# A landing semaphore for each expert slot, two expert loads in flight, and a published count for the engines

## The reference

```python
def moe(h, w_router, b_router, w_eg, w_eu, w_ed):
    scores = jax.nn.sigmoid(logits)            # logits = h @ w_router
    sel = scores + b_router
    grp_score = jnp.sum(lax.top_k(grp, TOP_K)[0], axis=-1)
    best = jnp.argmax(grp_score, axis=-1)      # one of 4 groups of 4 experts
    _, idx = lax.top_k(masked, TOP_K)          # two experts of that group
    ...
    gate = jnp.einsum('btd,edf->btef', h, w_eg)
    up = jnp.einsum('btd,edf->btef', h, w_eu)
    a = jax.nn.silu(gate) * up * combine[..., None]
    return jnp.einsum('btef,efd->btd', a, w_ed)
```

## Time and profile before

| | us |
|---|---|
| median of 3 runs | 1204.32 |
| lowest and highest | 1196.26, 1206.15 |
| the profiled execution | 1205.71 |
| its span, first to last instruction | 1203.7 |
| PE busy (share) | 1050.0 (87%) |
| DVE busy (share) | 670.2 (56%) |
| ACT busy (share) | 412.2 (34%) |
| POOL busy (share) | 202.6 (17%) |
| mean granted clock of TensorE | 0.927 |

### The profile page before, as it was taken

One profiled execution on the slowest core, in us unless ns is written; L12 is line 12 of the kernel. 1 busy time (PEld: TensorE's weight loads), 2 busy tenths in 40 slices (PEclk: granted clock), 3 DMA queues, 4 the chain that ended last, 5 costly groups with the idle time before them and its releaser, 6 DMA issues.

```text
span 1203.7 us, 18160 instructions
## 1 busy us (share of the span) xinstructions
PE 1050.0 (87%) x5952; PEld 798.1 (66%) x5953; DVE 670.2 (56%) x1125; ACT 412.2 (34%) x803; POOL 202.6 (17%) x244
## 2 busy tenths in 40 slices
PE   5899999999999999789878999983599989979950
PEld 2599999989999875569874555543366656646640
DVE  3431887141797138319985333356666766567644
ACT  3342322252222242535662101110244444344413
POOL 2200000000000021002354000000224324324324
PEclk9599999999999999799998999995699999989985
DMA  9543333223342132122125322208448888887848
GB/s 351 204 142 122 139 139 140 89 80 116 137 157 99 60 136 77 39 88 63 53 45 228 114 95 105 105 36 296 175 145 241 293 265 247 277 271 201 243 65 349
DMA packets 58643, 187.37 MB, mean 156 GB/s; under 512 B 7874, under 2 KB 20658, under 8 KB 52450
## 3 DMA queue, kind: packets, MB, share of 16 engines
q1 hardware_dynamic: 46100, 142.29, 33.0%
q0 software_dynamic: 7920, 28.84, 10.4%
q10 hardware_dynamic: 4576, 15.62, 3.4%
HBM read 151.53 MB, written 35.21 MB: 155 GB/s over the span
## 4 chain that ended last, share of the span: by engine, by line
PE 71%; DVE 13%; DMA 7%; issue 3%; ACT 3%; POOL 1%; ACTq 1%; SPq 0%; DVEq 0%; POOLq 0%
PE psum L1242 35%; PE psum L1184 27%; DMA RB<-in_w_exp 2%; PE psum L1461 2%; DVE RW L1725 2%; DMA RB<-in_x_sample 2%; PE psum L1123 2%; DVE RE L1752 1%; DMA acc_scratch<-RE,idxsc 1%; DMA out<-RB 1%; DVE RE L1760 1%; PE psum L1396 1%; PE psum L1199 1%; PE psum L1168 1%; DMA RW<-gm_scratch 1%
## 5 line engine op out<-in xcount | busy, mean ns | idle before, releaser
L1184 PE MATMUL psum<-input_parts,weight_parts 128*128 128x320 f32 x2208 | 340.9, 313 | 1.7 <-DVE input_parts L1560 1.7
L1184 PEld LDWEIGHTS psum<-input_parts,weight_parts 128*128 128x128 f32 x2208 | 326.9, 189 | 10.6 <-issue 6.9
L1242 PE MATMUL psum<-RB,RW 128*128 x324 | 147.9, 607 | 1.5 <-issue 1.3
L1567 DVE TENSOR_TENSOR weight_parts<-RW,weight_parts 128x1024 fp32r<-128x1024 f32 x46 | 56.3, 1224 | 164.8 <-ACT weight_parts L854 164.8
L854 ACT ACTIVATE weight_parts<-RW 128x1024 fp32r<-128x1024 f32 x46 | 48.7, 1058 | 238.2 <-PE psum L1184 238.0
L1242 PE MATMUL psum<-expert_parts 128*128 128x512 f32 x486 | 126.5, 413 | 1.9 <-DVE expert_parts L1989 1.9
L1242 PEld LDWEIGHTS psum<-expert_parts 128*128 128x128 f32 x486 | 91.3, 188 | 32.4 <-issue 14.8
L1242 PEld LDWEIGHTS psum<-RB,RW 128*128 128x128 f32 x324 | 61.2, 196 | 69.4 <-issue 69.4
L1242 PE MATMUL psum<-RS,RB 128*128 128x512 f32 (+1 forms) x200 | 79.9, 554 | 2.7 <-DMA RS<-in_wpw 1.5
L673 POOL TENSOR_TENSOR RE<-RE,RA 2x2304 f32<-2x2304 f32 (+1 forms) x2 | 9.5, 4762 | 404.9 <-DMA RA<-in_b_ada 404.9
L1242 PE MATMUL psum<-RC,RB 128*128 128x512 f32 x160 | 72.5, 607 | 0.0
(11 more groups left out here) (325 smaller groups left out, 1498.3 us busy)
## 6 DMA issues: line engine op xcount, KB each, us to landing
RB<-in_w_exp SPq DMA_DIRECT2D x48, 1024.0 KB
RW<-in_w_ada SPq DMA_DIRECT2D x48, 512.0 KB, 3.5
RW<-in_w_in SPq DMA_DIRECT2D x46, 512.0 KB, 4.1
RW<-gm_scratch SPq DMA_DIRECT2D x20, 256.0 KB, 3.4
h_scratch<-RE SPq DMA_DIRECT2D x10, 512.0 KB, 2.6
acc_scratch<-RA SPq DMA_DIRECT2D x10, 512.0 KB, 3.6
RB<-acc_scratch ACTq DMA_DIRECT2D x10, 512.0 KB, 7.3
out<-RB SPq DMA_DIRECT2D x10, 512.0 KB, 2.7
```

The lines of the kernel that those rows point to most:

```text
L1184: last = nc.tensor.matmul(psum[:, 2 * r + g, 0:GW], spl[:, r, wv, k], hT[:, xv, k, g * GW:(g + 1) * GW], start=(k == 0 and wv == 0 and xv ...
L1242: return nc.tensor.matmul(out, lhsT, rhs, start=start, stop=stop, **kw_)
L1567: nc.vector.tensor_tensor(spl[:, r, 1], raw[:, r], spl[:, r, 0].bitcast(F32), ALU.subtract).then_inc(wlo_ok, 1)
```

## The change

The three parts of a load now add to a semaphore of their slot, `w_land0` to `w_land2`. Nobody but SyncE waits on these. When SyncE finds that a slot's load has landed, it adds 48 to `w_full` by an empty instruction (`publish`). The other engines' code is unchanged: they wait on `w_full` as before. SyncE no longer waits for the landing of load n-1 before it issues load n, but issues load n when its slot is free and then waits for load n-1 and publishes it. Loads 0 and 1 are issued together; load 15 is followed by the publications of experts 14 and 15. The first pass of the loop is written out.

```diff
+    w_land = [sem(f"w_land{r}") for r in range(3)]
...
-        def load_expert(r, src, came):
-            if came is not None:
-                sp.wait_ge(w_full, came)
+        def load_expert(r, src):
             for q in range(WPART):
-                sp.dma_start(wexp[:, r * WE + q * WP:r * WE + (q + 1) * WP], src[:, q * WP:(q + 1) * WP]).then_inc(w_full, 16)
+                sp.dma_start(wexp[:, r * WE + q * WP:r * WE + (q + 1) * WP], src[:, q * WP:(q + 1) * WP]).then_inc(w_land[r], 16)
+
+        def publish(r, landed):
+            sp.wait_ge(w_land[r], landed)
+            nc.sync.nop().then_inc(w_full, 16 * WPART)
 
         sp.wait_ge(lg_ps, NT)
         for e in range(2):
-            load_expert(e, a["w_exp"][e], 16 * WPART * e if e else None)
+            load_expert(e, a["w_exp"][e])
+        publish(0, 16 * WPART)
         sp.wait_ge(route_ok, 3)
...
-        load_expert(2, listed(slice(2, 3)), 16 * WPART * 2)
-        with sp.Fori(1, NE // 3) as i:
+        load_expert(2, listed(slice(2, 3)))
+        publish(1, 16 * WPART)
+        publish(2, 16 * WPART)
+
+        def refill(n, free, r):
+            done = sp.value_load(endI[0:1, free], min_val=1, max_val=NBLK)
+            src = listed(n)
+            sp.wait_ge(dn_ps, done)
+            load_expert(r, src)
+
+        for r in range(3):
+            refill(slice(3 + r, 4 + r), slice(r, r + 1), r)
+            if r:
+                publish(r - 1, 2 * 16 * WPART)
+        with sp.Fori(2, NE // 3) as i:
             for r in range(3):
-                done = sp.value_load(endI[0:1, bass.ds(i * 3 + (r - 3), 1)], min_val=1, max_val=NBLK)
-                src = listed(bass.ds(i * 3 + r, 1))
-                sp.wait_ge(w_full, i * (48 * WPART) + 16 * WPART * r)
-                sp.wait_ge(dn_ps, done)
-                load_expert(r, src, None)
+                refill(bass.ds(i * 3 + r, 1), bass.ds(i * 3 + (r - 3), 1), r)
+                publish((r - 1) % 3, i * (16 * WPART) + (16 * WPART if r else 0))
         done = sp.value_load(endI[0:1, NE - 4:NE - 3], min_val=1, max_val=NBLK)
         src = listed(slice(NE - 1, NE))
         sp.wait_ge(dn_ps, done)
-        load_expert(0, src, 16 * WPART * (NE - 1))
+        load_expert(0, src)
+        publish(2, 5 * 16 * WPART)
+        publish(0, 6 * 16 * WPART)
```

## The result

The changed kernel took 1239.02 us, median of 4 runs (1234.78 to 1242.77), against 1200.29 us for the kernel before in the same comparison. The ratio is 1.0288, 95% interval 1.0246 to 1.0330: slower by some 35 us. A second comparison on another occasion gave 1.0301 (1.0235 to 1.0366), with medians of 1237.54 and 1203.49, 34.1 us apart.

A forecast was written before the change was run, and what follows sets the result against it. The MoE loop was taken as bound by TensorE. New stalls 28.5, plus 4.1 at expert 7, minus 0.7 at expert 11, gave +31.9 us: 1205.7 to 1237.6, for the median 1236; range 1227 to 1246.

The forecast's parts named there:

- Part 1: SyncE's loads in the MoE loop: removing the wait for the previous landing gains 0 on the path, at most 15.6 us.
- Part 2: Publication behind the next refill: TensorE idles 7.4 us at the transposes where the expert ahead has one block; +31.9 us overall.
- The block behind a stall: MoE loop: the next block after a stall runs 2.1 us over its 10.35 us period, bounds 1.3 and 2.6.
- Which experts: Experts with one-block predecessors pay: 4, 10, 13 by 9.5 us each, 7 by +4.1, 11 by -0.7.
- expert 2 spared: Before the loop: expert 2's publication follows its own load without a refill between, long before block 3 wants it; no cost.
- The pair at 10 and 11: Blocks 16, 17: expert 10's new stall lets load 11 land earlier; expert 11's stall costs 9.5 instead of 10.2, -0.7 us.
- A full stall: At a late block's transposes: 7.4 us idle plus 2.1 us for the slower next block, 9.5 us, between 8.5 and 11.1.
- the two old stalls: Kernel before, late landings of loads 7 and 11: stalls costing 5.4 and 10.2 us, 15.6 us together.
- The one without the clock: Rival at the loop's stalls: gaps come but the clock falls no more often than now; +26 us, 1230; chance 0.11.
- The one in which the clock stays low: Rival: the whole next block or more after each of five stalls runs at lower clock; 15 us on top, 1251; chance 0.08.

The follow-up runs named there:

- The seven late publications: Changed from the kernel before: experts 3, 5, 6, 8, 9, 12, 14 published behind the next load's issue, the loop written out; ratio 1.0016.
- the order ahead of the slot wait: Changed kernel with only the order moved: expert n-1 is published before SyncE waits for load n's slot; ratio 1.0010 to the kernel before.
- the slack experiment: Experts 5, 6, 8, 9, 14 published late, behind 3 or 8 more SyncE register loads; 1205.27 and 1213.58 us, kernel before 1201.21 to 1207.92.
- the experiment with expert 10 alone: Loop written out; against the kernel before, only expert 10 is published late; ratio 0.9997.
- slack_8: Late publication of experts 5, 6, 8, 9, 14, each behind eight more register loads on SyncE; 1213.58 us, kernel before 1201.21 to 1207.92.

## Why the prediction was right

**Where it bounded the kernel.** The blocks named, 6, 11, 16, 17 and 21, came late, and no others. All blocks that were neither late nor right behind a late one kept the period of 10.35 us, except the first, block 0, which takes 11.5 here and 11.6 in the kernel before.

**Part 1, no gain.** Right. The seven late publications, with loads 4, 6 and 15 free to go out earlier, give the time of before within 0.4%, and so does the order ahead of the slot wait.

**Part 2, the gap.** Forecast 7.4 us (2.06 to the gate weights, 5.36 of chain). Measured at block 6: 932.04 - 930.15 = 1.89 and 937.25 - 932.04 = 5.21, together 7.1; at block 16, 1055.14 to 1060.37, 5.23 of chain. What the trace before didn't show (a met wait, an empty instruction, a wake-up) took 0.20 us, from the end of the third DMA's issue at 931.84 to 932.04, where 0.3 was taken. Blocks 6, 11, 16 and 21 came 7.1 to 7.6 us late; block 17 came behind a slow block and can't be read by itself.

**The block behind a stall.** Forecast 2.1 over the period, measured 2.48 at block 6 and 2.52 at block 17 (12.83 and 12.87). The forecast put it all to the clock, and at these blocks that is right: 12.83 x 0.81 = 10.4 leaves nothing over. Put as a loss, an estimate from the length and the granted clock of the window, it is (1 - 0.81) x 12.83 = 2.4 us for block 6. In the kernel before, the blocks behind the second and the first stall had a granted clock of 0.83 and 0.87, an undisturbed one 1.00. The same estimate gives (1 - 0.83) x 12.46 = 2.1 us for the second stall, as measured, but (1 - 0.87) x 12.91 = 1.7 us for the first, where the row has 2.56. That last block has 12.91 - 12.26 = 0.65 us in which TensorE is idle, the same idle piece as behind the short waits of the slack experiment. With it the sum is 2.3 of the 2.56. What the idle piece waits for no trace here shows.

**Which experts, and the sum.** Experts 4, 7, 10, 11 and 13, with expert 2 spared: each as forecast. The pair at 10 and 11 behaved as reckoned, and the experiment with expert 10 alone showed the same rule from its other side. A full stall was forecast at 9.5 us and one alone measured 9.6 in the trace, 10.2 by the ratio. The sum was +31.9; the loops of the first two profiles differ by 32.4. Part of this closeness is luck: the stalls that were subtracted come from the very profile with which it is compared, and they differ between executions.

**What was off.** The median came out 3 us above the forecast (1239 against 1236) and the change at 35 us instead of 32. The term that was off most is what was subtracted for the two old stalls, 15.6 us. They end with landings: in the three profiles of the kernel before they cost 15.6, 10.3 and 14.7 us, 13.5 on average, so 2.1 us too much was taken off. The five new ones cost 48.7 us in the first profile of the changed kernel (7.1 + 2.5, 7.6 + 2.2, 7.3 + 9.7 + 2.5, 7.4 + 2.4, late and behind) against 5 x 9.5 = 47.5; the block behind a stall was the larger part of that. Against this stand small delays of 1.5 us on average in other blocks of the kernel before, which the changed kernel doesn't have. All this is about the loop; that it makes up the whole of the 35 us isn't shown.

**The rivals.** The one without the clock (1230) falls by the blocks behind, which were longer by a quarter. The one in which the clock stays low (1251) falls too, for the granted clock of 0.50 lasted some 4.75 us at block 6 and not a block; but it was priced too low. By the product of length and granted clock, 10.4 at block 6, a block that takes 10.35 us at 1.00 would take 10.35 / 0.50 = 20.7 at 0.50, some 10 us more and not 5, so that this rival stood for about 1276 (both are estimates; the second is 1236 and five times 8).

## What to carry to other kernels

When one queue both waits for free space and passes on news of arrivals, every consumer inherits the space wait: here ScalarE's waits for its gate weights went from 17.4 to 51.3 us. Ask of each signal what its sender waits for just ahead of it, and compare that with when the receiver wants it. Here the data had landed long before, and a counter bumped at the wrong place cost 3%. Issuing a load ahead of the landing before it can help only where that landing holds it back: here loads 4, 6 and 15, freed of waits of 0.6 to 1.6 us, gained nothing (1.0016). Where the slot holds it, freeing the slot in parts, at the last read of each part, gained 0.8% here.

## What the runs showed of the hardware

In the trace with eight register loads (`slack_8`), short waits of TensorE cost more than their own length although the granted clock of the block behind stayed at 1.00. Behind five waits of 1.2 to 1.7 us the next block took 0.97 to 1.08 us over its 10.35; 0.64 to 0.70 us of each is idle, and in the one shown TensorE waited in it for nothing that the profile shows. In the changed kernel, behind waits of 7 us the granted clock of the next block fell to 0.81 at block 6 and 0.80 at block 17: the first 4.75 us of block 6 ran at 0.50, and both blocks took about 2.5 us more. A register load on SyncE took 0.55 us (`slack_8`, eight in a row that start from 947.72 to 951.55).
